# The boundary between two layers with its norm split by token halves, and the first three tiles of the second layer taken half by half

## The reference

```python
# layer one, its end (o is the output of its attention branches)
o = jnp.concatenate([o_mla, o_fox], axis=-1) @ w_out
x = x + _rms_norm(o, g_post)                    # a norm over the 2048 channels of each token

# layer two, its beginning
h = _rmsnorm(x, norm_g[l])
proj = h @ w_in[l]                              # first the 512 columns kca, vca, for _compress
...
x = x + jnp.concatenate([y_a, y_b], axis=-1) @ w_out[l]
return _rmsnorm(x, final_g)
```

## Time and profile before

| | us |
|---|---|
| median of 3 executions (lowest, highest) | 1788.24 (1787.73, 1789.04) |
| the profiled execution, its own time | 1790.47 |
| its span in the profile | 1788.7 |
| TensorE busy | 1773.7 (99%) |
| VectorE busy | 1173.0 (66%) |
| ScalarE busy | 724.5 (41%) |

### The profile page before, as it was taken

How to read it: one execution, slowest core, us unless ns; L and a number is a source line. 1 busy time by engine, 2 the same in 40 slices (tenths; PEclk the granted TensorE clock), 3 DMA queues, 4 the chain that set the end, 5 groups by cost and what they waited for, 6 DMA issues and landing times.

```text
span 1788.7 us, 26190 instructions
## 1 busy us (share of the span) xinstructions
PE 1773.7 (99%) x9392; PEld 1514.0 (85%) x9392; DVE 1173.0 (66%) x2327; ACT 724.5 (41%) x1341; POOL 67.0 (4%) x89
## 2 busy tenths in 40 slices
PE   9999999999999999999999999999999999999997
PEld 7788888888888888889988887888888888888997
DVE  7444434444433788888878875767767667678786
ACT  6433323322222455544436243433434333454452
POOL 0000000000000000000002000000000000000122
PEclk9999999999999999999999999999999999999999
DMA  6444434432222333322348364221212222123434
GB/s 239 143 124 114 129 105 116 120 112 83 82 98 91 118 119 106 105 94 72 117 151 228 106 212 144 76 63 59 71 59 71 95 64 88 59 82 119 148 119 148
DMA packets 56917, 198.81 MB, mean 111 GB/s; under 512 B 6688, under 2 KB 7864, under 8 KB 56320
## 3 DMA queue, kind: packets, MB, share of 16 engines
q1 hardware_dynamic: 49968, 172.97, 30.1%
q0 software_dynamic: 6864, 24.69, 5.2%
HBM read 189.20 MB, written 8.43 MB: 110 GB/s over the span
## 4 chain that ended last, share of the span: by engine, by line
PE 92%; DVE 4%; DVEq 1%; ACT 1%; issue 1%; DMA 0%; SPq 0%; ACTq 0%
PE strip L560 21%; PE strip L562 20%; PE strip L561 20%; PE scores L560 5%; PE scores L561 5%; PE scores L562 5%; PE outputs L562 3%; PE outputs L561 3%; PE outputs L560 2%; PE scores L602 1%; PE scores L654 1%; PE scores L662 1%; PE scores L1106 1%; PE scores L658 1%; PE scores L1129 1%
## 5 line engine op out<-in xcount | busy, mean ns | idle before, releaser
L560 PE MATMUL strip<-xh,wh 128*128 128x512 f32 (+1 forms) x1704 | 658.8, 387 | 2.0 <-DVE xl L2229 1.2
L562 PE MATMUL strip<-xh,wl 128*128 128x512 f32 (+1 forms) x1704 | 650.4, 382 | 0.0
L561 PE MATMUL strip<-xl,wh 128*128 128x512 f32 (+1 forms) x1704 | 649.9, 381 | 0.0
L1826 DVE TENSOR_TENSOR wl<-raw,wh 128x1024 fp32r<-128x1024 f32 (+3 forms) x274 | 318.0, 1172 | 138.6 <-ACT wh L1219 137.6
L560 PEld LDWEIGHTS strip<-xh,wh 128*128 128x128 f32 x1704 | 320.6, 188 | 65.0 <-DVE xl L2229 2.1
L562 PEld LDWEIGHTS strip<-xh,wl 128*128 128x128 f32 x1704 | 320.4, 188 | 62.9
L561 PEld LDWEIGHTS strip<-xl,wh 128*128 128x128 f32 x1704 | 320.7, 188 | 59.2 <-issue 0.5
L1219 ACT ACTIVATE wh<-raw 128x1024 fp32r<-128x1024 f32 (+3 forms) x276 | 274.7, 1016 | 144.1 <-PE strip L562 98.8
L1241 ACT ACTIVATE prob<-prob,nms 128x128 f32<-128x128 f32 (+3 forms) x128 | 70.4, 551 | 101.8 <-DVE nms L1881 101.8
L1834 DVE TENSOR_TENSOR y<-strip,rb 128x512 f32<-128x512 f32 x47 | 32.5, 692 | 103.7 <-PE strip L562 101.5
L1524 ACT ACTIVATE wh<-raw 128x1024 fp32r<-128x1024 f32 x54 | 57.2, 1059 | 80.6 <-PE scores L562 27.6
(11 more groups left out here) (495 smaller groups left out, 2677.0 us busy)
## 6 DMA issues: line engine op xcount, KB each, us to landing
raw<-in_w SPq DMA_DIRECT2D x312, 512.0 KB, 3.6
mfox<-in_mfox POOLq DMA_DIRECT2D x8, 640.0 KB, 4.2
mfox<-decay POOLq DMA_DIRECT2D x8, 640.0 KB, 7.3
xn<-o POOLq DMA_DIRECT2D x4, 1024.0 KB, 7.8
o<-in_xt SPq DMA_DIRECT2D x7, 512.0 KB, 9.3
out<-oh SPq DMA_DIRECT2D x14, 256.0 KB, 2.8
o<-in_xt POOLq DMA_DIRECT2D x13, 256.0 KB, 6.5
o<-xn POOLq DMA_DIRECT2D x12, 256.0 KB, 3.4
```

Source lines behind the costliest of these rows:

```text
L560: pe.matmul(out, ah, bh, start=first, stop=False, skip_group_check=shared)
L561: pe.matmul(out, ah, bl, start=False, stop=False, skip_group_check=shared)
L562: return pe.matmul(out, al, bh, start=False, stop=last, skip_group_check=shared)
L1826: v_.tensor_tensor(wl[s][:, :cols], raw[s][:, :cols], wh[s][:, :cols].bitcast(F32), ALU.subtract)\
```

## The change

- The norm of layer one is made by token halves. The late half's squares are added within the last strip pair (`late_sq`, `late_square`). Its token sums stand in the middle of product 5 (`late_sums`), and the spread of its factors into `po` in the middle of product 6 (`late_spread`). The early half's sums follow the pair, and its spread stands within the second late tile, into the bank `pj[0]`, with both halves in it (`pe_whole_spread`).
- `pe_four` gets its first three tiles (`HALVED`) in another order: the tiles 0, 1, 2 of the late half, then those of the early half, 128x256 each. Tiles 3 to 15 are as before.
- The four matmuls of `acc` and `gate` whose results nobody reads are gone.
- Tile 3 gets its residual on VectorE too (`ADDED` = 4). GpSimd's queue loads x for it with the others, after product 3 instead of product 4 of the last pair, and the tables `cos2`, `sin2` right behind.
- `lo` of the units `U_CMPIN` + 2 and + 3 moves from ahead of the scaling to behind tile 6's.

```diff
-WARM_FIRST, WARM_MID, ADDED = 4, 2, 3
+WARM_FIRST, ADDED, HALVED = 4, 4, 3
...
-        g.wait_ge(w_used, conv(0, PAIRS[0] - 1, 5))
+        g.wait_ge(w_used, conv(0, PAIRS[0] - 1, 4))
         g.dma_start(xr1[:, :, :], d["xt"][:, 0:2, :]).then_inc(xr1_in, 16)
-        g.dma_start(xr1c[:, :, :], d["xt"][:, 2:3, :]).then_inc(xr1c_in, 16)
-        g.wait_ge(w_used, conv(0, PAIRS[0] - 1, 6))
+        g.dma_start(xr1c[:, :, :], d["xt"][:, 2:4, :]).then_inc(xr1c_in, 16)
         g.dma_start(cos2[:, :], d["cos_a"]).then_inc(tab2_in, 16)
         g.dma_start(sin2[:, :], d["sin_a"]).then_inc(tab2_in, 16)
         g.memset(blk[:, :, :], 0.0).then_inc(blk_zero, 1)
...
+            ins = pe.matmul(out[:, mine], ones[:, :], gate[:, mine], start=t == 2, stop=t == 3, skip_group_check=True)
...
+    def pe_whole_spread(pe, out):
+
+        for t in (2, 3, 0, 1):
+            mine = slice(P * t, P * t + P)
+            if t < 2:
+                pe.wait_ge(diag_done, NQ + 3 + t)
+            ins = pe.matmul(out[:, mine], ones[:, :], gate[:, mine], start=t == 2, stop=t == 1, skip_group_check=True)
+        ins.then_inc(spread, 1)
...
+            pe.wait_ge(acc_ready, 3)
+            for t in (2, 3):
+                ins = pe.matmul(px[:, t:t + 1], acc[:, P * t:P * t + P], ones[:, 0:1], start=t == 2, stop=t == 3,
+                                skip_group_check=True)
+            ins.then_inc(sum_done, 1)
...
-                product(w, q_, 5, by, False, *of_x(0, TOKENS[1]))
+                last = w == 0 and q_ == PAIRS[0] - 1
+                product(w, q_, 5, by, False, *of_x(0, TOKENS[1]), between=late_sums if last else None)
...
-                product(w, q_, 6, bx, False, *of_x(8, TOKENS[0]))
+                product(w, q_, 6, bx, False, *of_x(8, TOKENS[0]), between=late_spread if last else None)
 
         strip_pairs(0)
-        pe_token_sums(pe, 3, N_OUT1 + KT)
-        for i in range(2):
-            pe.matmul(sb[3][:, :], ones[:, :], acc[:, :], start=True, stop=True)
-        pe_spread(pe, 1, (po,))
-        for i in range(WARM_MID):
-            pe.matmul(px[:, :], ones[:, :], gate[:, :], start=True, stop=True)
-        pe_four(pe, U_CMPIN, 3 * KT - 6, sb, summed=(4, 0))
+        pe.wait_ge(acc_ready, 4)
+        for t in range(2):
+            pe.matmul(px[:, t:t + 1], acc[:, P * t:P * t + P], ones[:, 0:1], start=t == 0, stop=False,
+                      skip_group_check=True)
+        pe.wait_ge(ev_act, N_OUT1 + KT)
+        for t in range(2):
+            ins = pe.matmul(px[:, t:t + 1], e_t[:, P * t:P * t + P], ones[:, 0:1], start=False, stop=t == 1,
+                            skip_group_check=True)
+        ins.then_inc(sum_done, 1)
+
+        pe.wait_ge(y_done, N_OUT1 + KT)
+        pe.wait_ge(w_lo, U_CMPIN + 2)
+        for h, hi_done, lo_done, before in ((1, late_hi, late_lo, 0), (0, x_hi, x_lo, 3 * KT - 6)):
+            for j in range(HALVED):
+                slot, at_ = (U_CMPIN + j // 2) % SLOTS, 512 * (j % 2)
+                tile = xh[:, j, TOKENS[h]], xl[:, j, TOKENS[h]]
+                pe.wait_ge(hi_done, before + j + 1)
+                for part in (wh, wl):
+                    for s in range(4):
+                        pe.matmul(sb[s][:, TOKENS[h]], part[slot][:, at_ + P * s:at_ + P * s + P], tile[0],
+                                  start=h == 1 and j == 0 and part is wh, stop=False, skip_group_check=True)
+                if h == 1 and j == 1:
+                    pe_whole_spread(pe, pj[0])
+                pe.wait_ge(lo_done, before + j + 1)
+                for s in range(4):
+                    ins = pe.matmul(sb[s][:, TOKENS[h]], wh[slot][:, at_ + P * s:at_ + P * s + P], tile[1],
+                                    start=False, stop=False, skip_group_check=True)
+                if h == 0 and j == 1:
+                    ins.then_inc(w_used, 1)
+        pe_four(pe, U_CMPIN, 3 * KT - 6, sb, summed=(5, 0), done=HALVED)
+        pe.wait_ge(scaled, KT - ADDED)
...
+                if w == 0 and q_ == PAIRS[0] - 1:
+                    a.wait_ge(w_part, 3 * q_ + 3)
+                    a.activation(e_t[:, TOKENS[1]], o[:, 15, TOKENS[1]], ACT.Square).then_inc(late_sq, 1)
+                    a.wait_ge(late_added, 1)
+                    a.wait_ge(c12_out, PAIRS[0])
+                    a.activation(e_t[:, TOKENS[1]], o[:, 14, TOKENS[1]], ACT.Square).then_inc(late_sq, 1)
                 if w == 1 and q_ == PAIRS[1] - 1:
                     part_square(13, 1, w_part, 3 * (PAIRS[0] + q_) + 3)
                     a.wait_ge(r_done, N_OUT2 + 15)
                     part_square(12, 1, c12_out, PAIRS[0] + PAIRS[1])
                 pair_hi(w, q_ + 1, 0)
+                if w == 0 and q_ == PAIRS[0] - 1:
+                    act_root(a, 3, 2, 4)
...
-        a.wait_ge(r_done, N_OUT1 + KT - 1)
-        a.activation(e_t[:, TOKENS[1]], o[:, KT - 2, TOKENS[1]], ACT.Square)
+        a.wait_ge(late_added, 2)
+        part_square(15, 0, y_done, taken(0, 14))
+        a.wait_ge(r_done, taken(0, 14))
         a.wait_ge(w_used, conv(0, PAIRS[0] - 1, 8))
         a.activation(e_t[:, TOKENS[0]], pair_banks(0, PAIRS[0] - 1)[0][:, 0:256], ACT.Square).then_inc(ev_act, 1)
         first_block(PAIRS[0] - 1)
-        act_root(a, 3)
-        act_hi(a, At(U_CMPIN + 3))
...
+        def tile_hi(j):
+            a.wait_ge(xn_done, j + 1)
+            tokens = TOKENS[0] if j < HALVED else slice(0, S)
+            a.activation(xh[:, j, tokens], o[:, j, tokens], ACT.Copy, scale=c("g_2", j)).then_inc(x_hi, 1)
...
+        late_tile(0)
+        late_tile(1)
+        act_root(a, 4, 0, 2)
+        act_hi(a, At(U_CMPIN + 2))
+        late_tile(2)
+        act_hi(a, At(U_CMPIN + 3))
+        tile_hi(0)
+        tile_hi(1)
+        tile_square(0)
+        tile_hi(2)
+        tile_square(1)
+        tile_hi(3)
+        tile_square(2)
+        tile_square(3)
+        for j in range(ADDED, KT):
+            a.wait_ge(x_added[j % 4], 16 * (j // 4 + (j % 4 >= ADDED)))
+            a.activation(xh[:, j, :], o[:, j, :], ACT.Copy, scale=c("g_2", j)).then_inc(x_hi, 1)
+            tile_square(j)
...
+            v_.drain()
+            v_.wait_ge(late_sq, n_)
+            v_.tensor_tensor(acc[:, TOKENS[1]], acc[:, TOKENS[1]], e_t[:, TOKENS[1]], ALU.add).then_inc(late_added, 1)
...
+                else:
+                    late_square(1)
                 v_.wait_ge(w_used, conv(w, q_, 5))
                 whole_part(w, o[:, j, TOKENS[1]], bz, p16, c12_out)
                 if w == 1 and not more:
                     squared_half(1, taken(1, 13) - 4)
                     v_.drain().then_inc(acc_ready, 1)
+                if w == 0 and not more:
+                    late_square(2)
+                    v_.drain().then_inc(acc_ready, 1)
                 pair_lo(w, q_ + 1, 0)
+                if w == 0 and not more:
+                    token_rms(v_, 3, 2, 4)
...
-        squared(0, KT - 2)
+        squared_half(0, taken(0, 14))
         v_.drain().then_inc(acc_ready, 1)
         v_.drain().then_inc(r_done, 1)
-        lo(v_, At(U_CMPIN + 2))
-        token_rms(v_, 3)
-        lo(v_, At(U_CMPIN + 3))
-        v_.wait_ge(spread, 2)
...
         def scale_tile(j):
-            ins = v_.scalar_tensor_tensor(o[:, j, :], o[:, j, :], c("g_post", j), po[:, :], ALU.mult, ALU.mult)
...
+        def residual(j, tokens=slice(0, S), done=xn_done):
             v_.drain()
             v_.wait_ge(xr1_in if j < 2 else xr1c_in, 16)
-            v_.tensor_tensor(o[:, j, :], o[:, j, :], xr1[:, j, :] if j < 2 else xr1c[:, 0, :], ALU.add)\
-              .then_inc(xn_done, 1)
+            from_ = xr1 if j < 2 else xr1c
+            v_.tensor_tensor(o[:, j, tokens], o[:, j, tokens], from_[:, j % 2, tokens], ALU.add).then_inc(done, 1)
...
+        def scale_half(j, h):
+            v_.scalar_tensor_tensor(o[:, j, TOKENS[h]], o[:, j, TOKENS[h]], c("g_post", j),
...
+        def late_start(j):
+            scale_half(j, 1)
+            residual(j, TOKENS[1], xn_late)
+
+        def late_rest(j):
+            v_.wait_ge(late_hi, j + 1)
+            v_.scalar_tensor_tensor(xl[:, j, TOKENS[1]], o[:, j, TOKENS[1]], c("g_2", j),
+                                    xh[:, j, TOKENS[1]].bitcast(F32), ALU.mult, ALU.subtract).then_inc(late_lo, 1)
...
+        def early_start(j):
+            scale_half(j, 0)
+            residual(j, TOKENS[0])
...
-        scale_tile(0)
-        residual(0)
-        scale_tile(1)
-        residual(1)
+        v_.wait_ge(spread, 2)
+        late_start(0)
+        late_start(1)
+        late_rest(0)
+        token_rms(v_, 4, 0, 2)
+        late_rest(1)
+        late_start(2)
+        v_.wait_ge(spread, 3)
+        scale_tile(4)
+        early_start(0)
+        late_rest(2)
+        scale_tile(5)
+        early_start(1)
+        early_rest(0)
+        early_start(2)
+        early_rest(1)
         scale_tile(3)
-        new_rest(0)
-        scale_tile(2)
-        residual(2)
-        new_rest(1)
-        scale_tile(4)
-        new_rest(2)
```

(9 more changed lines are left out.)

82 lines of the change are left out of this document (43 added, 39 removed).

## The result

| | before | after |
|---|---|---|
| median of 22 executions each, us | 1788.87 | 1791.17 |
| lowest, highest | 1787.73, 1789.88 | 1789.03, 1793.66 |
| profiled execution: time, span | 1790.47, 1788.7 | 1792.93, 1791.1 |

The changed kernel takes 1.0013 of the time before, with a 95% interval of 1.0007 to 1.0019. That is 2.3 us slower: less than the 0.2% that counts as a change here, but outside the forecast range of 1784.8 to 1788.9, and of the other sign. The interval lies above 1.

The account below looks back on a forecast made before the run. TensorE's list bounds the kernel, VectorE's rations the boundary: of a 7.0 us earlier start 2.3 remain at tile 4, 1.6 after a 0.7 wait at the norm's sum; 1788.24 - 1.6 = 1786.6, range 1784.8 to 1788.9.

Parts of the forecast that it names:

- The base: Boundary times summed in the profiled execution (1790.47); the gain of 1.6 then taken off the median 1788.24, giving 1786.6.
- forecast of 946.05: Start of layer two's tile 4: TensorE waits for VectorE's xl until 946.05, against 948.39 now, 2.3 us gained.
- forecast sum at 973.5: Sum for layer two's norm: additions done at 973.5, TensorE there at 972.8, a wait up to 0.7, leaving 1.6.
- Costed at nothing: Larger xr1c load at the boundary, 256 KB more and one product earlier: priced at zero, at worst no gain.
- my neutral rival: Gain used up near the end or by one slow stretch, such as a 1.2 GHz clock in 928 to 931: 1788.1, 20%.
- The pair: Last strip pair: wait of 0.75 in product 5, 0.2 at the spread; ends at 926.5, not 924.8, 1.7 lost.
- VectorE's list: VectorE's work from first scaling at 926.8 to tile 4's xl: 19.2 us, ready at 946.0.
- the two bounds: At tile 4: VectorE's xl, ready at 946.0, and ScalarE's high part with hi and wl, ending at 945.9, 0.1 beside.
- Slower, by TensorE's clock: Clock falls within the last pair, about 923.4, and stays low until 937: 3.7 us behind, 1791.9, chance 7%.
- the first rival: VectorE does not hold the boundary; up to 6.0 us gained, 1782.2; chance 6%, 7% in the summary.
- the middle: Outcome within 0.2% (3.6 us), neither faster nor slower by more: 86% in the summary of 7%, 86%, 7%.
- 921.05: Late half's second square addition on VectorE in the last pair done at 921.05, from the copy-out at 918.38.

Follow-up runs that it names:

- e5: The kernel before, unchanged, profiled a second time: 1788.20 us in one execution, with the clock at 1.00 from 926 to 934.
- e1: The changed kernel run once more as it is: 1791.70 us, ratio 1.0016 to the kernel before.
- e14: The changed kernel with the tables' loads (and the memset behind them) moved back after product 5, x still early: 1790.29 us, ratio 1.0008.
- e2: The changed kernel with GpSimd's loads of x and tables back at their old places: 1790.13 us, ratio 1.0008 to the kernel before.
- e15: The changed kernel with GpSimd's loads at their old places and its memset of blk ahead of the loads of x: 1789.94 us, ratio 1.0006.
- e3: The kernel before without its four 128x512 matmuls whose results nobody reads: 1790.37 us, ratio 1.0011.
- e10: The kernel before with the four stores of the new x moved behind the last accumulating load: 1788.78 us, ratio 1.0001.
- e6: The kernel before, unchanged, profiled a third time: 1789.33 us in one execution, clocks 0.62 and 0.95.
- e13: The kernel before with GpSimd's loads issued early, x after product 3 and the tables right behind: 1793.12 us, ratio 1.0025.
- e17: e2 with the memset ahead of x's loads, tile 3 by DMA, two units' lo and tile 4's xh moved, stores late: 1787.85 us, ratio 0.9995.

## Why the prediction was wrong

**The base.** The step "the sum is made in the profiled execution … a difference of it is taken off the median" failed. The stretch to be saved was 935.33 minus the pair's end in that profile, and 933.05 to 933.84 in the others. Tile 4's last matmuls (wh\*xl) start at 948.39 there and at 945.96 in e5. My own forecast of 946.05 for the changed kernel is therefore a gain of 2.3 against the one and of nothing against the other. What was said of all executions (a clock of 0.60 and 0.55) was true of one. The base was mis-sized by up to 2.3. The sign of it was in my own figures: the 2.2 by which that execution lay above the median is nearly this whole stall. On e5 as base, the forecast sum at 973.5 is a loss of 0.8 against 972.71, and not a gain of 1.6.

**"Costed at nothing: the larger xr1c … at a DMA share that … is only 0.72 and 0.41".** This is the other step that failed. I priced the size of one load and read the DMA share from 926 on; what mattered was which loads stand ahead of the weight load at 918.29. In 918 to 922, where that load runs, the DMA share is 0.58 in before and 0.90 in after. The tables moved from 922.29 to 917.11, and x from 918.96, behind the weight load, to 916.06, ahead of it; the sum gave that order no price. Forecast: VectorE scales at 926.8. Measured 928.20, 1.4 later, behind a load of 6.82; in e1, 929.51. The load takes 5.7 with x alone early (e14) and 3.5 to 3.7 with neither. In e14 the delay is not seen in the scaling, since the diagonals hold VectorE in any case; with the tables early as well it is. The bound that I put on it ("at most until it now begins to scale, which leaves the outcome at no gain") left out that TensorE idles meanwhile and then runs at a low clock. That was the mechanism of my neutral rival, at its place: the clock falls in 930 to 934, VectorE stands 1.43 for the spread (2.2 in the rival). Together with the 1.4 this is 2.8 of the 2.9 by which the sum at 976.43 missed the forecast 973.5. The trace of after names the cause; e2, in which both waits are gone at once, bears it out, with the memset's 1.04 newly in the pair.

**The pair.** Right. The wait in product 5 was forecast at 0.75 and is 0.56; the spread was given 0.2 of wait and has none in after and e15. The pair's last matmul starts at 926.28 in after, against a forecast end of 926.5. But this price holds only where GpSimd's memset doesn't stand beside the diagonals: 1.04 in e2.

**VectorE's list.** Right, and closely. 19.2 from the first scaling to tile 4's `xl`; after has 948.28 + 0.75 - 928.20 - 1.43 (the wait) = 19.40. In the profiled execution of e15, where neither loads nor memset disturb, the terms stand at their forecast places: scaling 926.69 (926.8), first late tile 928.36 (928.35), a wait of 1.29 at tile 4, its wh\*xl matmuls at 946.04 (946.05), the sum with a wait of 0.50 at 973.61 (973.5). TensorE waits for `xh` there, and its wh\*xl matmuls start 0.05 behind the end of `xl` (945.99): the two bounds are as close as the 0.1 that I gave them.

**The gain then.** VectorE scales 3.9 earlier in e15 than in e5 (8.36 against 12.27). From there to the end of tile 4's `xl` it is 19.3 in e15 (926.69 to 945.99) and 13.1 in e5 (930.64 to 943.73): VectorE has 6.2 more ahead of it, among it the halves, the early half's `token_rms` and the `lo` of two units that stood beside the unread matmuls. In e5 it was 2.2 ahead of TensorE there. The earlier start and that lead together, 6.1, are used up at tile 4, whose wh\*xl matmuls start 27.71 behind the copy-out in e15 and 27.59 in e5. Behind it e15 loses 0.8 more, 0.5 of it the wait ahead of the sum (55.28 and 54.34). The medians agree: e15 is 0.95 above its kernel before, with an interval that reaches from 0.5 below to 2.7 above. So without the disturbances the change, in its forecast places, still gains nothing that was measured.

**The rivals.** "Slower, by TensorE's clock" had the sign right and the place wrong: it wanted the clock to fall within the pair, and all profiles of changed kernels have 1.00 up to at least 926. The throttled state as default, which the Trainium skill (TensorE: Matmul & The Clock Gate, Part 1: The HAM clock gate) names, agrees with e3: the four unread matmuls, taken out alone, cost 2.0. I had read the low clock beside them as a sign that they don't hold it up; in e5 and e10 the clock is 1.00 beside them, in the first profile and in e6 it isn't. Two small slips change nothing: the first rival has 6% in its own paragraph and 7% in the summary, where the middle should then be 87%; and 921.05 should be 921.04.

**Open.** The time behind the boundary isn't settled. Near 1676 us VectorE stands for a weight load by 2.71 in after, 0.87 to 2.02 in all of its variants, and 0.37 to 0.53 in five profiles of the kernel before and its variants e3 and e10; e13 has 0.93. By the mark set for e13 (over 0.8) the early loads are a cause of it, but e2, with the loads at their old places, has 1.82, so they are not the only one. TensorE stands 1.4 behind it in after's profile (waits of 0.93 and 0.54), 0.9 in e2, e14 and e17, and not at all in e15. From the sum to the end of the span it is 814.67 in after, 813.95 in e2, 812.99 in e15, and 813.7 to 814.0 in the three profiles of before. Which order brings it about wasn't found. The changed kernel with the unread matmuls kept, which might hold its clock up in 930 to 934, was not run. Why the clock in the same program is 1.00 in one execution and 0.60 in another isn't known either.

## What to carry to other kernels

Profile the kernel before more than once and look at the granted clock at the place of the change: a stall seen in one execution may be the clock's, and an edit can't gain it from the median. When a DMA is issued earlier, ask which other load it now stands ahead of and who waits for that, and read the DMA share where that load runs. And when work is handed to a free queue, look at everything behind it in that list: here a memset of 1 us, moved unnoticed with the loads, cost 1.2 in the way to the first scaling, where the late weight load cost 1.5 to 2.3. One delay can hide another, as the memset hid the late load in e14: look at each wait, and not only at the time.

## What was not expected of the hardware

- A 512 KB weight load took 3.5 to 3.7 us from issue to landing with x and the tables issued behind it, 5.7 with 1 MB of x issued about 2 us ahead of it, and 6.0 to 7.7 with 0.5 MB of tables between x (0.75 or 1 MB) and it. In the changed kernel ScalarE stood 0.98 for it in the second case, and 2.09 and 2.95 in the third.
- Two 128x128 diagonals on VectorE (a scalar multiply) take 0.48, and 1.70 beside a GpSimd memset of 0.98. A 128x1024 subtraction of two tensors beside the same memset in the kernel before takes 1.23, and 1.22 without it. The Trainium skill (SBUF — State Buffer, Who interferes with whom) says that VectorE's `tensor_scalar` can take the port pair that it shares with GpSimd, that of two such instructions the one that issues first holds the pair for its whole length while the other blocks, and that an instruction with two SBUF inputs contends only with a GpSimd instruction that reads. The rows agree in that the diagonals end 0.14 behind the memset's end in e2, and in that the subtraction isn't slower. They don't show the order: by the profile the first diagonal starts 0.58 ahead of the memset and is held all the same.
- The same program's clock in 926 to 930 and in 930 to 934 was 1.00 and 1.00, 0.62 and 0.95, or 0.60 and 0.55; its way to the sum was 54.34, 55.41 and 56.60.
